# Group B's attention: which engine scales the first softmax map of each pair

## The chip, the cores and the metric

The kernel runs on one core of one Trainium2 chip. The metric is the device time of one execution in microseconds (us), the median of several runs. A core has five engines that matter here: TensorE (PE, with its weight loads as PEld), VectorE (DVE), ScalarE (ACT), GpSimd (POOL) and SyncE (SP), whose queue starts most of the DMAs. Each engine runs its own list of instructions in order and waits on semaphores for the others.

## The reference, cut to what matters

Two layers of an encoder step are computed for 1024 prompt frames (chunk-causal, chunks of 64) and 32 new frames behind 512 cached ones. Four head groups A, B, C and M read the same normed input. The change is in group B, differential attention: 4 heads, two softmax maps of 32-dim queries and keys for each head, 64-dim values.

```
ob = _full_attend(bq, bk, jnp.repeat(bv, 2, axis=2), B_SUB ** -0.5, q_start, prompt)
ob = ob.reshape(B, S, B_HEADS, 2, HEAD_DIM)
lam = exp(sum(lq1 * lk1)) - exp(sum(lq2 * lk2)) + lam_init
ob = _rms(ob[..., 0, :] - lam * ob[..., 1, :], b_subln_g) * (1.0 - lam_init)
```

So the output of a head is `softmax(map 0) @ v - lam * softmax(map 1) @ v`. The kernel forms the difference of the maps first, `P0 / sum0 - lam * P1 / sum1`, and multiplies it with the values once.

## The kernel before, in words

The kernel is a sequence of blocks with a barrier of all engines between them (`end_of_block`, L194). In each layer the groups M, B, A and C follow each other, each as a projection block (`pieces_block`) and an attention block (`attention_block`, L1004). Group B's attention runs twice, once in each layer.

An attention block goes through a list of jobs. For group B, `single_jobs` (L1294) makes 72 jobs: for each of the 8 prompt tiles of 128 frames, and for the tile of the 32 new frames, 8 jobs, one for each map. Jobs 2i and 2i+1 are the two maps of one head, a pair; there are 36 pairs in a layer. A job's keys are 128, 256, ... 1024 for the prompt tiles (4 pairs of each length) and 544 for the last tile (4 pairs). The order of work is written out by hand, one program for each engine, tied by semaphores:

- PE (L1076): scores of job j+2 (L1089), which wait until ScalarE has read the PSUM banks that they go to. Jobs of at most 512 keys have four such places and longer ones two. After an odd job it transposes the finished map of the pair (`turn`, L1104) and multiplies the transposed map of the pair before with the values (`values`, L1121).
- DVE (L1140): the mask and the negated row maximum of job j+1 (`maximum`, L1153 and L1163), then `divide(j)`. For an even job, `divide` is one reciprocal of the row sum (L1174), which signals `map_den`. For an odd job it is a reciprocal (L1183), a product with minus lambda (L1184), and, after a wait for `map_scaled`, the combination of both maps (L1186), which signals `p_ready`. Then comes the copy of an older output (`out_copy`, L1206).
- ACT (L1234): in an even step j, the exponential of job j+1 with its row sum (L1247), the scaling of map j (L1275, after a wait for `map_den`), the copies of the transposed maps from PSUM (L1263), and in the next step the exponential of job j+2.
- POOL (L1224): only for jobs of four heads (groups M and A) does it scale the maps (L1230). In group B's attention its program is empty.
- SP (L1281): sends each output tile to DRAM.

The tiles: `prob` holds the maps of four jobs, `rden` the reciprocals (element 0 of row 0 for the first map, of row 1 for the second), `pt` the transposed maps, `osb` the outputs, `nm` the negated maxima.

Of the kernel before, what the change touches and what calls it, by code (L numbers as in the profile page):

```python
# [19 lines left out]
ALU = mybir.AluOpType  # L20
# [24 lines left out]
def build_program(nc, I, O, consts):  # L45
# [958 lines left out]
    def attention_block(jobs, v_of, products, nk, start, pt_start=None, sinks=False, diff=False):  # L1004
# [7 lines left out]
        prob = w.take("prob", [P, 4, 1024])  # L1012
# [5 lines left out]
        rden = w.take("rden", [P, 2, 4])  # L1018
        osb = w.take("osb", [P, 4, 2 * P])
        NJ = len(jobs)  # L1020
# [3 lines left out]
        def segs(j):  # L1024

            jb = jobs[j]
            out = []
            for i in range(len(jb["heads"])):
                c = 0
                while c < jb["keys"]:  # L1030
                    n = min(P, jb["keys"] - c)
                    out.append((i, jb["tile0"] + c // P, i * 256 + c, n))
                    c += n
            return out

        def turn_groups(j):

            out, cur = [], []
            for n, sg in enumerate(segs(j)):
                if cur and (len(cur) == 4 or segs(j)[cur[0]][3] != sg[3]):  # L1040
                    out.append(cur)
                    cur = []
                cur.append(n)
            out.append(cur)
            return out
# [14 lines left out]
        def banks(j):  # L1060
            return [j % 4] if short(j) else [2 * (j % 2), 2 * (j % 2) + 1]
# [12 lines left out]
        with nc.Block() as block:  # L1074
            @block.tensor
            def _(pe):  # L1076
# [16 lines left out]
                def turn(p):  # L1093
                    j = pv_jobs[p]
                    r = jobs[j]["rows"]
                    pe.wait_ge(S.p_ready, p + 1)
                    sg = segs(j)
                    for n, grp in enumerate(turn_groups(j)):
                        g = first_group[p] + n
                        if g >= 2:  # L1100
                            pe.wait_ge(S.pt_copied, g - 1)
                        for i, b in enumerate(grp):
                            _, _, col, kn = sg[b]
                            last = pe.transpose(ps[0:kn, 4 + g % 2, i * P:i * P + r], prob[0:r, j % 4, col:col + kn],  # L1104
                                                ident[0:r, 0:r])
                        last.then_inc(S.pt_done, 1)

                def values(p):
                    j = pv_jobs[p]
                    r = jobs[j]["rows"]  # L1110
                    pe.wait_ge(S.pt_copied, first_group[p + 1])
                    if p >= 2:
                        pe.wait_ge(S.o_copied, p - 1)
                    sg = segs(j)
                    for i, h in enumerate(jobs[j]["heads"]):
                        mine = [n for n, x in enumerate(sg) if x[0] == i]
                        hp = jobs[j]["v_heads"][i]
                        part = 64 * (hp[0] % 2)
                        for m, b in enumerate(mine):
                            _, kt, _, kn = sg[b]  # L1120
                            last = pe.matmul(ps[part:part + 64, 6 + p % 2, (i // 2) * P:(i // 2) * P + r],  # L1121
                                             v_of(kt)[0:kn, 64 * hp[1]:64 * hp[1] + 64], pt[0:kn, p % 2, b, 0:r],
                                             start=(m == 0), stop=(m == len(mine) - 1))
                    last.then_inc(S.pv_done, 1)
# [98 lines left out]
            @block.gpsimd  # L1223
            def _(pool):  # L1224
                for j in range(NJ):
                    r, kn, nh = jobs[j]["rows"], jobs[j]["keys"], len(jobs[j]["heads"])
                    if nh > 1:
                        pool.wait_ge(S.den_ready, j + 1)
                        v = prob[0:r, j % 4, :].rearrange("p (h c) -> p h c", c=256)[:, :, 0:kn]
                        pool.tensor_tensor(v, v, rden[0:r, j % 2, 0:nh].unsqueeze(2).broadcast_to([r, nh, kn]),  # L1230
                                           ALU.mult).then_inc(S.p_ready, 1)

            @block.scalar
            def _(act):  # L1234
                def exponent(j):
                    jb = jobs[j]
                    r, kn, nh = jb["rows"], jb["keys"], len(jb["heads"])
                    act.wait_ge(S.nm_done, j + 1)
                    if j >= 4:
                        if diff and j % 2 == 0:  # L1240
                            act.wait_ge(S.p_ready, (j - 4) // 2 + 1)
                        else:
                            act.wait_ge(S.pt_done, first_group[sum(1 for q in pv_jobs if q <= j - 4)])
                    for i in range(nh):
                        col = i * 256
                        src = ps[0:r, banks(j)[0]:banks(j)[-1] + 1, :].rearrange("p a b -> p (a b)")[:, col:col + kn]
                        last = act.activation(prob[0:r, j % 4, col:col + kn], src, ACT.Exp, bias=nm[0:r, j % 4, i:i + 1],  # L1247
                                              accum_out=rsum[0:r, j % 4, i:i + 1])
                    if sinks:
                        last = act.activation(es[0:r, j % 2, :], es[0:r, j % 2, :], ACT.Exp)  # L1250
                    last.then_inc(S.exp_done, 1)

                def turned_copy(p):
                    j = pv_jobs[p]
                    r = jobs[j]["rows"]
                    sg = segs(j)
                    if p >= 2:
                        act.wait_ge(S.pv_done, p - 1)
                    for n, grp in enumerate(turn_groups(j)):
                        g = first_group[p] + n  # L1260
                        act.wait_ge(S.pt_done, g + 1)
                        kn = sg[grp[0]][3]
                        act.copy(pt[0:kn, p % 2, grp[0]:grp[0] + len(grp), 0:r],  # L1263
                                 ps[0:kn, 4 + g % 2, 0:len(grp) * P].rearrange("p (m c) -> p m c", c=P)[:, :, 0:r]
                                 ).then_inc(S.pt_copied, 1)

                exponent(0)
                p = 0
                for j in range(NJ + 1):
                    if j + 1 < NJ:  # L1270
                        exponent(j + 1)
                    if diff and j < NJ and j % 2 == 0:
                        r, kn = jobs[j]["rows"], jobs[j]["keys"]
                        act.wait_ge(S.map_den, j // 2 + 1)
                        act.mul(prob[0:r, j % 4, 0:kn], prob[0:r, j % 4, 0:kn], rden[0:r, 0, 0:1]).then_inc(S.map_scaled, 1)  # L1275
                    if p < NPV and pv_jobs[p] == j - 1:
                        turned_copy(p)
                        p += 1
# [864 lines left out]
```

## Time and profile before

| | |
|---|---|
| time, median of 3 runs (lowest to highest) | 3410.72 us (3407.08 to 3412.3) |
| span of the profiled execution | 3406.1 us |
| PE busy | 2985.7 us (88%) |
| PEld busy | 2776.2 us (82%) |
| DVE busy | 1793.5 us (53%) |
| ACT busy | 1407.6 us (41%) |
| POOL busy | 163.9 us (5%), 238 instructions |

The page gives the span of the profiled execution, from its first to its last instruction; no time of its own beside that span is given for it. The span is 4.6 us below the median. Shares are averages over all stages. Group B's attention is a stage of about 133 us in each layer, from 276.3 to 409.1 us and from 1949 to 2082 us; what ends last there has to be read from its own rows.

### The profile page before, as it was taken

The page shows a single profiled execution, that of the slowest core. Times are in us where ns is not written, and L with a number is a line of the kernel's source. Part 1 is how long each engine was busy: PE and PEld are TensorE (multiplying, and loading weights), DVE is VectorE, ACT ScalarE, POOL GpSimd, SP SyncE. Part 2 cuts the span into 40 slices and gives each one's busy share as a digit, 9 for nine tenths or more (in the row PEclk, how much of TensorE's full clock was granted, in tenths as well). Part 3 has the DMA queues.
Part 4 walks back from the last instruction along what each step waited for, and adds up shares of the span by engine and source line. Part 5 has one row for each costly group of instructions (what it writes and reads, how often), then busy time and mean ns, then how long its engine had stood idle before and what let it go on. Part 6 is the DMA issues. An engine that isn't in the chain of part 4 may idle for free. (4 is left out here: it accounts for less than half of the span.)

```text
span 3406.1 us, 50141 instructions
## 1 busy us (share of the span) xinstructions
PE 2985.7 (88%) x19244; PEld 2776.2 (82%) x19244; DVE 1793.5 (53%) x2837; ACT 1407.6 (41%) x2909; POOL 163.9 (5%) x238
## 2 busy tenths in 40 slices
PE   5787788797899999999967877797888999999997
PEld 3785577486799999999957856675687999999997
DVE  5366664664545444444564586456456444454444
ACT  5556644653242233222245575546423223222332
POOL 0100002100000000000002000120000000000000
PEclk8898889897899999999988998897998999999998
DMA  4110102004011111111031101110221111111111
GB/s 174 38 42 18 33 7 56 5 12 153 25 50 44 50 45 44 44 44 50 19 119 45 45 10 31 32 34 6 68 92 44 50 44 44 44 44 50 45 44 59
DMA packets 185839, 162.22 MB, mean 48 GB/s; under 512 B 17272, under 2 KB 172408, under 8 KB 185080
## 3 DMA queue, kind: packets, MB, share of 16 engines
q1 hardware_dynamic: 185592, 158.82, 14.9%
q8 instruction: 169, 2.77, 0.3%
q14 instruction: 78, 0.64, 0.1%
HBM read 129.92 MB, written 29.06 MB: 47 GB/s over the span
## 5 line engine op out<-in xcount | busy, mean ns | idle before, releaser
L1500 PE MATMUL ps<-h_hi,w_hi 128*128 128x352 f32 x2496 | 545.8, 327 | 50.3 <-DVE h_lo L317 22.6
L1500 PE MATMUL ps<-h_lo,w_hi 128*128 128x352 f32 x2496 | 541.6, 325 | 0.0
L1500 PE MATMUL ps<-h_hi,w_lo 128*128 128x352 f32 x2496 | 541.4, 324 | 0.0
L1500 PEld LDWEIGHTS ps<-h_hi,w_hi 128*128 128x128 f32 x2496 | 428.1, 190 | 57.6 <-issue 43.2
L1500 PEld LDWEIGHTS ps<-h_hi,w_lo 128*128 128x128 f32 x2496 | 431.6, 189 | 0.0
L1500 PEld LDWEIGHTS ps<-h_lo,w_hi 128*128 128x128 f32 x2496 | 428.3, 190 | 0.0
L697 PE MATMUL ps<-w_hi,h_hi 128*128 128x256 f32 (+1 forms) x1152 | 337.7, 293 | 68.8 <-DVE w_lo L853 64.0
L2004 DVE TENSOR_TENSOR x_t<-ps,x_t 128x1056 f32<-128x1056 f32 x176 | 221.0, 1255 | 289.5 <-PE ps L1500 288.8
L1980 DVE SCALAR_TENSOR_TENSOR cv<-up,cols,cv 128x1058 f32<-128x1058 f32 x88 | 116.1, 1319 | 477.7 <-ACT cv L1919 477.7
L698 PE MATMUL ps<-w_lo,h_hi 128*128 128x256 f32 (+1 forms) x1152 | 332.7, 289 | 0.0
L699 PE MATMUL ps<-w_hi,h_lo 128*128 128x256 f32 (+1 forms) x1152 | 330.4, 287 | 0.0
L1912 ACT COPY up<-ps 128x704 f32<-128x704 f32 x88 | 65.7, 746 | 591.4 <-PE ps L1500 591.4
L697 PEld LDWEIGHTS ps<-w_hi,h_hi 128*128 128x128 f32 (+1 forms) x1152 | 215.3, 187 | 73.3 <-DVE w_lo L853 48.4
L1089 PE MATMUL ps<-k_st,q_st 128*128 128x256 f32 (+9 forms) x768 | 195.8, 388 | 66.1 <-ACT prob L1247 44.5
L1247 ACT ACTIVATE prob<-ps,nm 128x256 f32<-128x256 f32 (+8 forms) x360 | 224.8, 638 | 58.9 <-DVE nm L1163 46.5
L1901 ACT CAST w_hi<-stage 128x1024 fp32r<-128x1024 f32 x132 | 135.9, 1043 | 241.5 <-PE ps L1500 240.8
L1500 PE MATMUL ps<-act_hi,w_hi 128*128 128x352 f32 x1056 | 229.4, 325 | 5.1 <-issue 5.1
L1500 PE MATMUL ps<-act_hi,w_lo 128*128 128x352 f32 x1056 | 229.0, 324 | 0.0
L1500 PE MATMUL ps<-act_lo,w_hi 128*128 128x352 f32 x1056 | 228.5, 325 | 0.0
L1089 PEld LDWEIGHTS ps<-k_st,q_st 128*128 128x128 f32 (+2 forms) x768 | 132.4, 225 | 113.2 <-ACT prob L1247 57.1
L699 PEld LDWEIGHTS ps<-w_hi,h_lo 128*128 128x128 f32 (+1 forms) x1152 | 216.0, 188 | 0.9
L698 PEld LDWEIGHTS ps<-w_lo,h_hi 128*128 128x128 f32 (+1 forms) x1152 | 215.3, 187 | 0.7
(174 smaller groups left out, 4555.7 us busy)
## 6 DMA issues: line engine op xcount, KB each, us to landing
stage<-in_f_win SPq DMA_DIRECT2D x88, 512.0 KB, 3.8
stage<-in_f_wout SPq DMA_DIRECT2D x44, 512.0 KB, 3.6
stage<-in_w_in SPq DMA_DIRECT2D x64, 256.0 KB, 4.0
x_spill<-x_t SPq DMA_DIRECT2D x2, 4224.0 KB, 13.7
o_in<-o_spill SPq DMA_DIRECT2D x8, 1056.0 KB, 9.4
x_t<-x_spill SPq DMA_DIRECT2D x2, 4224.0 KB
stage<-in_w_o SPq DMA_DIRECT2D x16, 512.0 KB, 5.2
x_in<-in_x_prompt SPq DMA_DIRECT2D x1, 4096.0 KB, 13.4
```

The costliest lines, as they stand in the source:

```text
L697: pe.matmul(out, h_hi[:, k, c:c + r], w_hi[:, k, :], start=(k == 0), stop=False)
L698: pe.matmul(out, h_hi[:, k, c:c + r], w_lo[:, k, :], start=False, stop=False)
L699: last = pe.matmul(out, h_lo[:, k, c:c + r], w_hi[:, k, :], start=False, stop=(k == KC - 1))
L1089: last = pe.matmul(out, q_st[0:nk, qb, q0:q0 + r], jb["k"][0:nk, jb["k_blk"] + kb, k0 + c:k0 + c + n], start=(m == 0), stop=(m == len(pair ...
L1247: last = act.activation(prob[0:r, j % 4, col:col + kn], src, ACT.Exp, bias=nm[0:r, j % 4, i:i + 1], accum_out=rsum[0:r, j % 4, i:i + 1])
L1500: last = pe.matmul(ps[:, s0 + b, 0:BAND], lh, rh_[:, b * BAND:(b + 1) * BAND], start=(first_k and n == 0), stop=(last_k and n == 2))
L1901: act.copy(w_hi[:, ws, :], stage[:, sg, :]).then_inc(S.hi_done, 1)
L1912: act.copy(up[:, b, 2:2 + 2 * BAND].rearrange("p (t c) -> p t c", c=BAND), ps[:, s0:s0 + 2, 0:BAND])
L1980: dve.scalar_tensor_tensor(cv[:, b, :], up[:, b, 1:UPC - 1], cols[:, 0, bass.ds(c + 2 * FC, 1)], cv[:, b, :], ALU.mult, ALU.add).then_inc( ...
L2004: dve.tensor_tensor(xm, ps[:, s0:s0 + 3, 0:BAND], xm, ALU.add).then_inc(S.x_added, 1)
```

## The change

The scaling of the first map of each pair moves from ScalarE's program to GpSimd's, as a `tensor_scalar` with the per-row reciprocal as its operand. It waits for the same semaphore and signals the same one. Nothing else is changed.

```diff
@@ pool program
                 for j in range(NJ):
                     r, kn, nh = jobs[j]["rows"], jobs[j]["keys"], len(jobs[j]["heads"])
+                    if diff and j % 2 == 0:
+                        pool.wait_ge(S.map_den, j // 2 + 1)
+                        pool.tensor_scalar(prob[0:r, j % 4, 0:kn], prob[0:r, j % 4, 0:kn], rden[0:r, 0, 0:1], None,
+                                           ALU.mult).then_inc(S.map_scaled, 1)
                     if nh > 1:
@@ act program
                     if j + 1 < NJ:
                         exponent(j + 1)
-                    if diff and j < NJ and j % 2 == 0:
-                        r, kn = jobs[j]["rows"], jobs[j]["keys"]
-                        act.wait_ge(S.map_den, j // 2 + 1)
-                        act.mul(prob[0:r, j % 4, 0:kn], prob[0:r, j % 4, 0:kn], rden[0:r, 0, 0:1]).then_inc(S.map_scaled, 1)
                     if p < NPV and pv_jobs[p] == j - 1:
```

## Rows read from the trace of the kernel before

**Rows 1.** Waits of DVE in B's attention, first layer: engine, line, waited-for, total us, times, longest.
```profile
DVE prob L1186 <- ACT prob L1275: 9.9, 20, 0.7
```
**Rows 2.** The same in B's attention of the second layer.
```profile
DVE prob L1186 <- ACT prob L1275: 10.0, 20, 0.8
```
**Rows 3.** Timeline, one pair of 1024 keys: start, us, engine, line, operation [idle before <-releaser].
```profile
376.15 1.22 DVE L1163 TENSOR_REDUCE nm<-ps 128x1 f32<-128x1024 f32 x1
376.29 0.74 PE L1089 MATMUL ps<-k_st,q_st 128*128 128x512 f32 x2 [1.40 <-ACT prob L1247]
...
377.29 0.15 DVE L1174 RECIPROCAL rden<-rsum 128x1 f32<-128x1 f32 x1
377.41 1.11 ACT L1247 ACTIVATE prob<-ps,nm 128x1024 f32<-128x1024 f32 x1 [1.17 <-DVE nm L1163]
...
377.59 1.23 DVE L1163 TENSOR_REDUCE nm<-ps 128x1 f32<-128x1024 f32 x1
...
378.51 1.14 ACT L1275 ACTIVATE prob<-prob,rden 128x1024 f32<-128x1024 f32 x1
...
378.92 0.16 DVE L1184 TENSOR_TENSOR rden<-rden,neglam 128x1 f32<-128x1 f32 x1
...
379.75 1.28 DVE L1186 SCALAR_TENSOR_TENSOR prob<-prob,rden 128x1024 f32<-128x1024 f32 x1 [0.67 <-ACT prob L1275]
380.49 1.13 ACT L1247 ACTIVATE prob<-ps,nm 128x1024 f32<-128x1024 f32 x1
...
381.51 1.22 DVE L1163 TENSOR_REDUCE nm<-ps 128x1 f32<-128x1024 f32 x1
```
**Rows 4.** Timeline, one pair of 512 keys.
```profile
312.82 0.15 DVE L1174 RECIPROCAL rden<-rsum 128x1 f32<-128x1 f32 x1
...
313.12 0.69 DVE L1163 TENSOR_REDUCE nm<-ps 128x1 f32<-128x512 f32 x1
...
313.92 0.16 DVE L1184 TENSOR_TENSOR rden<-rden,neglam 128x1 f32<-128x1 f32 x1
...
314.11 0.75 DVE L1186 SCALAR_TENSOR_TENSOR prob<-prob,rden 128x512 f32<-128x512 f32 x1
```
**Rows 5.** GpSimd's groups by shape: busy us, mean ns of one | idle before.
```profile
L1230 POOL TENSOR_TENSOR prob<-prob,rden 128x1024 f32<-128x1024 f32 x30 | 56.8, 1893 | 156.5 <-DVE rden L1179 156.5
L317 POOL TENSOR_TENSOR h_lo<-h,h_hi 128x1056 fp32r<-128x1056 f32 x12 | 29.2, 2432 | 187.9 <-ACT h_hi L312 187.9
...
L222 POOL TENSOR_SCALAR_AFFINE_SELECT ident<-ident 128x128 f32<-128x128 f32 x1 | 0.3, 292 | 0.2 <-POOL ident L220 0.2
...
L1797 POOL COPY conv_st<-up 128x4 f32 x80 | 15.2, 190 | 1343.8 <-ACT up L1915 1343.8
...
L1230 POOL TENSOR_TENSOR prob<-prob,rden 128x512 f32<-128x512 f32 x2 | 2.1, 1040 | 688.6 <-DVE rden L1179 688.6
```
**Rows 6.** Timeline, group M's attention: a reciprocal and the GpSimd scaling behind it.
```profile
130.85 0.18 DVE L1179 RECIPROCAL rden<-rsum 128x4 f32<-128x4 f32 x1 [0.29 <-ACT prob L1247]
...
131.11 1.89 POOL L1230 TENSOR_TENSOR prob<-prob,rden 128x1024 f32<-128x1024 f32 x1 [63.16 <-DVE rden L1179]
```
**Rows 7.** Timeline of GpSimd, group A's attention, second layer.
```profile
2191.90 1.89 POOL L1230 TENSOR_TENSOR prob<-prob,rden 128x1024 f32<-128x1024 f32 x1 [1.20 <-DVE rden L1179]
```
**Rows 8.** Timeline of DVE in the same stretch.
```profile
2191.18 0.16 DVE L1160 TENSOR_TENSOR nm<-mx,negsink 128x4 f32<-128x4 f32 x1
...
2192.89 0.92 DVE L1160 TENSOR_TENSOR nm<-mx,negsink 32x4 f32<-32x4 f32 x1
```
**Rows 9.** Timeline, first pairs of the 32-frame tile.
```profile
395.25 0.43 PE L1089 MATMUL ps<-k_s,q_st 128*32 128x512 f32 x2
...
395.72 0.71 DVE L1163 TENSOR_REDUCE nm<-ps 32x1 f32<-32x544 f32 x1 [0.34 <-PE ps L1089]
```
**Rows 10.** Timeline, end of B's attention and start of group A's projections.
```profile
412.25 2.08 SPq L622 DMA_DIRECT2D stage<-in_w_in  x4
...
415.10 1.30 ACT L747 CAST w_hi<-stage 128x512 fp32r<-128x512 f32 x2 [8.50 <-DMA stage<-in_w_in]
```
**Rows 11.** Instructions of line L222: ns min/median/max, first and last start.
```profile
L222 POOLq MODIFY_POOL_CONFIG  x2: 11/11/11, 1.1 to 1.1; - x2
```

## The prediction

> **What bounds the kernel now.** The page's busy shares say little: PE is busy 88% of the span, but the change touches two stages of 133 us each. I first asked the waits of DVE in group B's attention, then a timeline of one pair of long keys and of one of short keys, then GpSimd's rows by shape, and last what stands around the stage.
>
> The waits show one thing to look for: DVE's combination of the two maps (L1186) waits for ScalarE's scaling (L1275) in 20 of the 36 pairs of a layer, 9.9 us in the first layer and 10.0 us in the second [rows 1, 2]. The 20 are the pairs of 640, 768, 896, 1024 and 544 keys; in the 16 pairs of up to 512 keys it doesn't wait.
>
> In a pair of 1024 keys [rows 3] the period from maximum to maximum is 381.51 - 376.15 = 5.36 us. The cycle that sets it runs over two engines: maximum on DVE (376.15 to 377.37), exponential of the second map on ACT (377.41 to 378.52), scaling on ACT (378.51 to 379.65), combination on DVE (379.75 to 381.03), an output copy and a mask, and the next maximum. DVE's own list is otherwise without a gap, and it sits idle only 0.67 us before the combination. The scaling could have started much earlier: its reciprocal is done at 377.29 + 0.15 = 377.44, but ACT's program puts the exponential, 1.11 us, ahead of it. PE isn't the bound: it waits 1.40 us in the same pair for ScalarE to free the banks.
>
> In a pair of 512 keys [rows 4] the combination starts 0.03 us after the product with minus lambda ends (313.92 + 0.16 = 314.08, start 314.11). DVE alone sets the period there, and taking work from ACT buys nothing.
>
> **The change part by part.** It removes one ACT instruction and its wait from each of 72 pairs, and adds one GpSimd instruction to each. ACT's time by itself is worth nothing, since ACT isn't the bound; what counts is when the scaled map is ready.
>
> *What goes.* Without the wait, the combination starts 0.03 us after the product, as in the short pairs. What it waited includes this 0.03 us, so the stall that can go is 9.9 + 10.0 - 40 x 0.03 = 18.7 us. The exponential and the copies of transposed maps on ACT move up by the scaling's 1.14 us at 1024 keys; nobody late waits for them.
>
> *What is added.* GpSimd has nothing else in this stage. Its scaling starts when the first reciprocal is done. In group M the same handover took 131.11 - (130.85 + 0.18) = 0.08 us [rows 6]. At 1024 keys GpSimd would start at 377.44 + 0.08 = 377.52, while DVE makes the maximum of the next job, the second reciprocal and the product. The product starts at 378.92, so the cover is 1.40 us, which is that reduce (1.22) plus 0.18. At 512 keys it is 313.92 - 312.97 - 0.08 = 0.87 us, again the reduce (0.69) plus 0.18 [rows 4]. The reduce grows by (1.22 - 0.69) / 512 = 1.04 ns an element from 0.16 us, so the cover is 0.34 + 1.04 n, with n in thousands of keys. The combination can start 0.19 us after the product started; the handover from ACT takes 0.10 us (379.65 to 379.75), and I take the same for GpSimd. So the scaling may last 0.09 us longer than the cover before anything is late.
>
> *How long it lasts* is not in the trace: no GpSimd `tensor_scalar` with a per-row operand is there. From the rows, one bound is the two-input product on the same tile (L1230): 1893 ns at 1024 elements and 1040 at 512, that is 0.187 us + 1.67 ns an element [rows 5]. The dearer two-input row is L317, (2.43 - 0.19) / 1056 = 2.1 ns an element. The other side are the one-input rows: a copy of 4 elements takes 190 ns and the affine select of 128 takes 292, which is (292 - 190) / 124 = 0.82 ns an element. The new instruction reads one tile and a single scalar for each row, so the one-input rows are nearest, and I take 0.187 us + 0.82 to 1.2 ns an element: 1.03 to 1.42 us at 1024, against 1.49 allowed; 0.60 to 0.80 at 512, against 0.96; 0.29 to 0.34 at 128, against 0.56. Nothing is late. In general the scaling is late by (r - 1.04) n - 0.24 us at r ns an element, so up to r = 1.27 it costs nothing at any length. Below nothing it can't go: what is hidden can't be hidden more.
>
> The page "GPSIMD Engine Reference" of the Trainium skill (section Engine selection) says the same kind of thing: one-input elementwise work is roughly at line rate on GpSimd, two-input work about twice as slow as on VectorE. For two inputs the trace shows 1.89 us on GpSimd (L1230) against 1.28 on VectorE (L1186) at 1024 elements [rows 3, 5], 1.5 times; no row here shows GpSimd's `tensor_scalar`.
>
> *A port.* A DVE instruction with two SBUF inputs stood still beside GpSimd here: L1160 takes 0.16 us when GpSimd is idle, and 0.92 us, from 2192.89 to 2193.81, when GpSimd's L1230 runs from 2191.90 to 2193.79 [rows 7, 8]. The Trainium skill's page "SBUF — State Buffer" (section Who interferes with whom) has this as a lock: such an instruction and a GpSimd instruction that reads SBUF exclude each other, and the second one waits to the end. The product L1184 has two SBUF inputs too. If the scaling ends before it starts, as at the price that I take, it costs nothing. If the scaling is still running, the product ends about 0.02 us after it and the combination starts 0.03 us later, no later than by the 0.10 us of the handover. So the lock adds nothing to the formula. The combination itself never meets a scaling, as it waits for one and the next starts only behind the next maximum.
>
> *What is late next.* With the 0.64 us gone at 1024 keys, the period is 4.72 us, DVE's own work. PE had 1.40 us of idle in 5.36 and keeps 0.76. ACT's second exponential moves up with the removed scaling: it started at 380.49 and would start at about 379.5, so the scores behind it are done before the maximum that needs them. Only at the step to the 32-frame tile does PE bind: DVE already waits 0.34 us there for scores that PE puts behind the value products of the 1024-key tile [rows 9]. There the gain of one pair, about 0.35 us in each layer, is not had: 0.7 us in both.
>
> *What follows.* A barrier ends the stage, the weights of group A are only requested at 412.25 and ACT waits 8.50 us for them [rows 10]. All of that starts from the end of the stage and moves up whole.
>
> *The sum:* 18.7 - 0.7 = 18.0 us. The sum is made against the profiled span: 3406.1 - 18.0 = 3388.1. The median of the runs is 4.6 us above that span, and I take the step off it: 3410.7 - 18.0 = 3392.7, said as 3393.
>
> **Rivals.**
> 1. GpSimd's `tensor_scalar` costs as much as its two-input product, 1.67 ns an element. Then the lateness 0.63 n - 0.24 is 0.40, 0.32, 0.24, 0.16, 0.10 and 0.08 us at 1024, 896, 768, 640, 544 and 512 keys, together 1.30 us, times 8 pairs each is 10.4 us. Gain 18.0 - 10.4 = 7.6, time 3403. For it: the only large GpSimd rows on this tile are of this price. Against: they read two tensors, and the one-input rows have half the slope.
> 2. The stall is replaced at once by another, PE or ACT being nearly as late as the scaling: time unchanged, 3410.7. For it: two bank places only for long jobs, and PE occupied for 3.96 us of the 5.36. Against: PE's idle of 1.40 us is over twice the 0.64 taken away, and ACT loses more work than the cycle loses time.
> 3. Slower: the instruction on GpSimd is so slow that DVE waits for it longer than it did for ACT, and also in the pairs of 256 to 512 keys, which wait for nothing today. The point from which this decides is r where the lateness, summed over 384 to 1024 keys and 8 pairs each, eats 18.7 us: 8 x (4.77 (r - 1.04) - 1.68) = 18.7, r = 1.88. At the rate of L317, 2.1, the lateness 1.06 n - 0.24 sums to 3.4 us over the eight lengths that have one, times 8 is 27.3 us: 8.6 us slower, 3419. For it: that row exists, 2.43 us. Against: it writes another number type and reads two full tensors.
> 4. The instruction needs other code on GpSimd. The trace shows a configuration step ahead of the affine select, 11 ns on the queue at 1.1 us, with the select running at 1.2 us [rows 5, 11]: 0.1 us, nothing in the sum. The Trainium skill's page "GPSIMD Engine Reference" (section Instruction dispatch) gives about 6 us for the first call of a freshly loaded library; by that, an estimate, two stages would give back 12 us. The rows show copies, fills and products running without such a step, and I leave it inside the range.
>
> **Numbers.** Chances: forecast 0.62, rival 1 0.18, rival 2 0.10, rival 3 0.07, rival 4 0.03. A measurement of this kernel tells some 0.2%, 6.8 us, from no change, so faster means below 3403.9. Faster: 0.62 + 0.13 of rival 1 = 0.75. Same: 0.05 + 0.10 + 0.03 = 0.18. Slower: 0.07. The forecast by itself lies between 3388 (a little more than the stall, as ACT's copies come earlier) and 3398 (some pairs late by 0.1 us). The range takes in rival 1 and half of rival 2: 3387 to 3409.
>
> **What would show it.** In the profile of the changed kernel the waits of DVE in this stage should have no row of L1186 for GpSimd, or one under 1 us; the period at 1024 keys should be 4.7 us; GpSimd's new rows at 1024 keys should be under 1.49 us, starting 0.08 us after the first reciprocal; L1184 should stay at 0.16 us. Each stage should be 9 us shorter and nothing else should move. A GpSimd row of 1.9 us at 1024 keys with L1184 stretched to its end would be rival 1; over 2.1 us, rival 3. A new wait of L1163 for PE in most pairs would be rival 2.

## The result, and the profile after

The changed kernel takes 3438.7 us (median of 4 runs, 3437.5 to 3441.5) against 3411.4 us for the kernel before beside it. The ratio on record is 1.0088, with a 95% interval from 1.0074 to 1.0102: 25 to 35 us slower. (The quotient of these two medians is 1.0080, or 27 us; the ratios below, too, are those on record and not quotients of the medians shown.) The prediction said 3393, with a range of 3387 to 3409. It was wrong in size and in sign.

In the profile the span is 3437.5 us, 31.4 us more than before. All of it lies in the two stages of group B's attention. Measured from DVE's first maximum to the end of its last output copy, these took 132.3 us each before; now they take 148.3 and 147.4 us, 31.2 us more together before rounding. The rest of the span is 3141.5 us before and 3141.7 after.

The waits of DVE in the two stages (engine, line, waited-for, total us, times, longest) answer to [rows 1, 2]. First the first layer:

```profile
DVE prob L1186 <- POOL prob L1229: 25.5, 31, 1.5
DVE ps L1153 <- PE ps L1089: 4.5, 1, 4.5
```

and the second layer:

```profile
DVE prob L1186 <- POOL prob L1229: 25.5, 31, 1.5
DVE ps L1153 <- PE ps L1089: 4.3, 1, 4.3
```

The combination's wait for ScalarE is gone, as meant. In its place it waits for GpSimd, in 31 pairs of a layer where 20 waited before, and 25.5 us where it was 9.9 or 10.0. 51.0 - 19.9 = 31.1 us: the new waiting is the whole loss. (The row of L1153 is the wait for the first scores and lies ahead of the stage as measured here.)

The timeline of one pair of 1024 keys in the changed kernel (start, us, engine, line, operation) answers to [rows 3]. ScalarE's exponential is now at line L1251.

```profile
386.36 1.22 DVE L1163 TENSOR_REDUCE nm<-ps 128x1 f32<-128x1024 f32 x1
...
387.50 0.15 DVE L1174 RECIPROCAL rden<-rsum 128x1 f32<-128x1 f32 x1
387.62 1.11 ACT L1251 ACTIVATE prob<-ps,nm 128x1024 f32<-128x1024 f32 x1 [2.94 <-DVE nm L1163]
...
387.75 2.84 POOL L1229 TENSOR_SCALAR prob<-prob,rden 128x1024 f32<-128x1024 f32 x1 [3.26 <-DVE rden L1174]
...
389.14 0.16 DVE L1184 TENSOR_TENSOR rden<-rden,neglam 128x1 f32<-128x1 f32 x1
...
390.70 1.28 DVE L1186 SCALAR_TENSOR_TENSOR prob<-prob,rden 128x1024 f32<-128x1024 f32 x1 [1.40 <-POOL prob L1229]
...
392.46 1.23 DVE L1163 TENSOR_REDUCE nm<-ps 128x1 f32<-128x1024 f32 x1
```

GpSimd starts 0.10 us after the reciprocal, well ahead of where ScalarE started, and then takes 2.84 us for what ScalarE did in 1.14. It ends at 390.59, and DVE has been idle since its product ended at 389.30. The period is 392.46 - 386.36 = 6.10 us, where it was 5.36. ScalarE has more idle time than before (2.94 us ahead of the exponential, 1.17 in [rows 3]), and it buys nothing.

GpSimd's new groups by shape (busy us, mean ns of one | idle before) answer to [rows 5]:

```profile
L1229 POOL TENSOR_SCALAR prob<-prob,rden 128x1024 f32<-128x1024 f32 x8 | 22.7, 2842 | 25.8 <-DVE rden L1174 25.8
L1229 POOL TENSOR_SCALAR prob<-prob,rden 128x896 f32<-128x896 f32 x8 | 20.2, 2522 | 23.7 <-DVE rden L1174 23.7
...
L1229 POOL TENSOR_SCALAR prob<-prob,rden 128x512 f32<-128x512 f32 x8 | 12.5, 1563 | 15.8 <-DVE rden L1174 15.8
...
L1229 POOL TENSOR_SCALAR prob<-prob,rden 128x128 f32<-128x128 f32 x8 | 4.8, 603 | 254.2 <-DVE rden L1174 254.2
```

Two of these give the price: (2842 - 603) / 896 = 2.50 ns an element, with 0.28 us fixed. That is dearer than either price that the prediction drew from the trace for a rival, 1.67 and 2.1.

What follows the stage moved as a block: the weights of group A are requested at 426.68, where it was 412.25, and ScalarE again waits 8.5 us for them.

### The profile page after: what moved, and what is told of

It reads as the page before. It is cut to its first block and busy times, and to the rows that moved or that the text cites. A ratio compares the mean times of both kernels' runs of the same rounds, so it can differ in the third digit from the quotient of the medians.

```text
span 3437.5 us, 50141 instructions
## 1 busy us (share of the span) xinstructions
PE 3014.0 (88%) x19244; PEld 2790.5 (81%) x19244; DVE 1793.8 (52%) x2837; ACT 1364.0 (40%) x2837; POOL 287.2 (8%) x310
## 3 DMA queue, kind: packets, MB, share of 16 engines
q8 instruction: 169, 2.77, 0.3%
## 5 line engine op out<-in xcount | busy, mean ns | idle before, releaser
L1251 ACT ACTIVATE prob<-ps,nm 128x256 f32<-128x256 f32 (+8 forms) x360 | 225.2, 638 | 115.0 <-DVE nm L1163 101.2
```

## The experiments

Ten kernels were run. "Stage" is the length of the stage as above, in the profile of each; it was worked out for both layers and is 132.3 us before. It is the sharpest measure here, as the rest of the kernel differs by up to 13 us between the profiles, from 3139.4 us (e10_copy2) to 3152.3 (e4_copy). Times are medians, and the kernel before ran beside each. e2_quarter, e4_copy and e10_copy2 leave out part or all of the scaling and e3_const scales by a wrong number, so these four compute another result; the others are complete kernels.

| run | GpSimd at 1024 keys | stage, us | us | ratio to before (95%) |
|---|---|---|---|---|
| changed kernel | 2.84 | 148.3, 147.4 | 3438.7 | 1.0088 (1.0074 to 1.0102) |
| e1_tt | 1.89 | 127.6, 127.6 | 3401.6 | 0.998 (0.997 to 0.999) |
| e2_quarter | 0.92 | 123.0, 123.0 | 3394.7 | 0.9955 (0.9939 to 0.9972) |
| e3_const | 2.77 | 145.6, 144.5 | 3434.5 | one run |
| e4_copy | 1.04 | 123.1, 123.0 | 3400.2 | one run |
| e5_early | 2.84 | 126.6, 126.5 | 3396.8 | 0.9969 (0.9957 to 0.998) |
| e6_early_tt | 1.89 | 126.0, 126.1 | 3396.3 | 0.9965 (0.9951 to 0.9979) |
| e7_early_act | none | 127.3, 127.1 | 3398.9 | 0.9971 (0.996 to 0.9983) |
| e8_split | 1.56, half | 125.9, 126.1 | 3396.6 | 0.997 (0.9959 to 0.9981) |
| e9_split_tt | 1.47, three quarters | 123.5, 123.3 | 3390.3 | 0.9957 (0.9943 to 0.9971) |
| e10_copy2 | 2 x 1.04 | 134.4, 134.5 | 3410.1 | one run |

The theory to test was that the whole loss is the duration of one instruction, and that the rest of the prediction (which stall goes, what covers the scaling, what is late next) stands. The rival was that GpSimd beside DVE costs time whatever it does.

### Another instruction for the same product (e1_tt)

```diff
-pool.tensor_scalar(prob[0:r, j % 4, 0:kn], prob[0:r, j % 4, 0:kn], rden[0:r, 0, 0:1], None,
-                   ALU.mult).then_inc(S.map_scaled, 1)
+pool.tensor_tensor(prob[0:r, j % 4, 0:kn], prob[0:r, j % 4, 0:kn],
+                   rden[0:r, 0, 0:1].broadcast_to([r, kn]), ALU.mult).then_inc(S.map_scaled, 1)
```

> The changed kernel with GpSimd's tensor_scalar replaced by its two-input product (tensor_tensor, the reciprocal broadcast along the row), at the same place and with the same semaphores. Theory (the loss is the price of the one instruction: its rows read 0.283 us + 2.50 ns an element, 2.84 us at 1024): at 0.187 + 1.67 ns an element, 1.89 us at 1024, the combination is late by 0.63 n - 0.24 us, so the kernel is 8 us faster than before, 3403, with DVE's waits at L1186 near 11 us over both layers. If the port lock seen at L1160 holds for L1184 too, L1184 is stretched to the end of GpSimd's product (its row about 0.5 us at 1024 in place of 0.16), with no further cost. Rival (work on GpSimd beside DVE costs whatever the instruction, through the handovers or the shared port): still slower than before, 3420 or more, and DVE's other rows in the stage longer.

One call was changed, for the same result, and the kernel went from some 30 us slower to faster than before, by 0.1 to 0.3%; 9.4 us less over the two stages against 8 expected. The rival falls: work on GpSimd in this place isn't a cost by itself. DVE's long instructions keep their durations, too: in the first layer the maximum takes 751 or 752 ns and the combination 813 ns on average in every run here. Only L1184 is longer, 259 ns on average in place of 158. The expected wait of 11 us at L1186 was not there in name, as the port took it. The rows of one 1024-key pair:

```profile
371.85 1.22 DVE L1163 TENSOR_REDUCE nm<-ps 128x1 f32<-128x1024 f32 x1
...
373.22 1.89 POOL L1229 TENSOR_TENSOR prob<-prob,rden 128x1024 f32<-128x1024 f32 x1 [3.25 <-DVE rden L1174]
...
374.62 0.51 DVE L1184 TENSOR_TENSOR rden<-rden,neglam 128x1 f32<-128x1 f32 x1
...
375.21 1.28 DVE L1186 SCALAR_TENSOR_TENSOR prob<-prob,rden 128x1024 f32<-128x1024 f32 x1
...
376.98 1.22 DVE L1163 TENSOR_REDUCE nm<-ps 128x1 f32<-128x1024 f32 x1
```

The product L1184 lasts until 375.13 (0.16 us otherwise), GpSimd's until 375.11. The wait for the scaled map now sits inside a busy row of 0.51 us instead of in an idle gap, so the list of waits shows none of it.

### A quarter of the columns (e2_quarter)

```diff
+kq = kn // 4
-pool.tensor_scalar(prob[0:r, j % 4, 0:kn], prob[0:r, j % 4, 0:kn], rden[0:r, 0, 0:1], None,
+pool.tensor_scalar(prob[0:r, j % 4, 0:kq], prob[0:r, j % 4, 0:kq], rden[0:r, 0, 0:1], None,
```

> The changed kernel with only the first quarter of each map's columns scaled on GpSimd (the rest of the map stays unscaled, work left out). Theory (once the scaling is shorter than its cover nothing is late): at 2.5 ns an element it lasts 0.283 + 0.64 = 0.92 us at 1024 keys, under the 1.49 allowed, so the whole 18.0 us of the prediction's sum are there: 3393, period at 1024 keys 4.72 us, no wait of L1186 for GpSimd. Rival (another wait takes the stall's place at once, PE's scores or ACT's exponentials): 3405 to 3411, with new DVE waits for PE or ACT of 10 us or more in the two stages.

The stages are 9.3 us shorter each, 18.7 us together. The time is 15 us less by the ratio (10 to 21), and the sum of the prediction, 18.0, lies in that interval. There is no wait at L1186, and the period at 1024 keys is 378.18 - 373.44 = 4.74 us:

```profile
373.44 1.23 DVE L1163 TENSOR_REDUCE nm<-ps 128x1 f32<-128x1024 f32 x1
...
374.83 0.93 POOL L1230 TENSOR_SCALAR prob<-prob,rden 128x256 f32<-128x256 f32 x1 [3.81 <-DVE rden L1174]
...
376.41 1.28 DVE L1186 SCALAR_TENSOR_TENSOR prob<-prob,rden 128x1024 f32<-128x1024 f32 x1
...
378.18 1.22 DVE L1163 TENSOR_REDUCE nm<-ps 128x1 f32<-128x1024 f32 x1
```

So the rest of the prediction holds: which stall goes, that DVE's own 4.7 us is the next limit, and that neither PE nor ACT takes its place.

### What makes tensor_scalar dear (e3_const, e4_copy)

```diff
# e3_const
-pool.tensor_scalar(prob[0:r, j % 4, 0:kn], prob[0:r, j % 4, 0:kn], rden[0:r, 0, 0:1], None,
+pool.tensor_scalar(prob[0:r, j % 4, 0:kn], prob[0:r, j % 4, 0:kn], 0.5, None,
# e4_copy
-pool.tensor_scalar(prob[0:r, j % 4, 0:kn], prob[0:r, j % 4, 0:kn], rden[0:r, 0, 0:1], None,
-                   ALU.mult).then_inc(S.map_scaled, 1)
+pool.tensor_copy(prob[0:r, j % 4, 0:kn], prob[0:r, j % 4, 0:kn]).then_inc(S.map_scaled, 1)
```

> The changed kernel with a constant 0.5 in place of the per-row reciprocal as GpSimd's operand (the first map is scaled by the wrong number). Theory (the price is the per-row operand, read again for every element beside the tile): the slope falls from 2.50 to about 1.7 ns an element or less, 1.9 us or less at 1024, and the kernel comes to about 3403 or lower. Rival (the price is tensor_scalar's own loop with its two operation slots): rows as in the changed kernel, 2.84 us at 1024, and 3438.

> The changed kernel with a plain one-input copy of each map onto itself on GpSimd in place of the scaling (no scaling at all, work left out). Theory of the prediction, kept for copies: one-input rows go at 0.82 ns an element, 1.03 us at 1024, and the kernel at 3393. Rival (no elementwise GpSimd instruction on this tile is faster than the product): 1.67 ns an element or more, 1.9 us or more at 1024, and 3403 or later. It tells whether the one-input rows were too small to be drawn out to 1024 elements, or whether tensor_scalar is the exception.

GpSimd's groups with the constant:

```profile
L1229 POOL TENSOR_SCALAR prob<-prob 128x1024 f32<-128x1024 f32 x8 | 22.2, 2770 | 25.7 <-DVE rden L1174 25.7
...
L1229 POOL TENSOR_SCALAR prob<-prob 128x128 f32<-128x128 f32 x8 | 4.2, 531 | 257.4 <-DVE rden L1174 257.4
```

and with the copy:

```profile
L1229 POOL COPY prob<-prob 128x1024 f32<-128x1024 f32 x8 | 8.3, 1042 | 29.5 <-DVE rden L1174 29.5
...
L1229 POOL COPY prob<-prob 128x128 f32<-128x128 f32 x8 | 2.4, 295 | 256.7 <-DVE rden L1174 256.7
```

The theory on the operand falls: reading it costs 0.07 us an instruction and nothing an element, the slope stays (2770 - 531) / 896 = 2.50 ns. The copy has (1042 - 295) / 896 = 0.83 ns and 0.19 us fixed, which is what the prediction had drawn from a copy of 4 elements and a select of 128. So the line through the small rows was good, for copies. It was the wrong instruction's line. Three instructions of GpSimd on the same tile cost 0.83 (copy), 1.67 (product of two tensors) and 2.50 ns an element (`tensor_scalar`), 1 to 2 to 3. Why the one with fewer inputs is the slower of the two products was not settled.

e4_copy's one execution took 3400.2 us where 3393 was expected, although its stages are 18.5 us shorter. The rest of that execution is 10.8 us longer than in the profile of before; why is not known, and it lies outside the change.

### An earlier start (e5_early, e6_early_tt)

```diff
 for j in range(NJ):
+    if diff and j % 2 == 0 and j:
+        divide(j)
     while seen <= upto(j, 1):
         maximum(seen)
         seen += 1
-    divide(j)
+    if not diff or j % 2 == 1 or j == 0:
+        divide(j)
```

> The changed kernel (tensor_scalar on GpSimd) with one move on DVE: the reciprocal of an even job is made before the maximum of the next job, not after it. Theory (the loss is only that the scaling outlasts its cover): GpSimd starts one reduce earlier, the cover grows to two reduces, the combination could start 0.90 + 2.08 n us behind the reciprocal and the scaled map is there at 0.46 + 2.50 n, which is never later up to 1024 keys. So the loss is gone and the stall of before too: 17 us faster than before, 3394, period at 1024 keys 4.75 us with the 2.84 us rows of GpSimd unchanged. A small new wait of DVE at the reciprocal for ACT's exponential, about 0.1 us a pair, may take 3 to 7 us of it. Rival (GpSimd's long instructions slow DVE down by themselves, through the shared port): still no faster than before, 3411 or more.

> Both: the two-input product on GpSimd and the reciprocal ahead of the next maximum. Theory: nothing is late and L1184 no longer meets GpSimd (product 1.89 us against some 2.8 us to L1184), so its rows are back at 0.16 us, and the time is that of the run before this one within 2 us, 3393, as GpSimd's speed no longer counts. Rival: if the instruction's speed counts still, it is faster than the tensor_scalar variant by 5 us or more.

With the slow `tensor_scalar` in place, 2.84 us as in the changed kernel, moving one reciprocal on DVE turns 31 us of loss over the stages into a gain of 11.4 us. The rival falls: GpSimd may be as slow as that if its cover is long enough. One pair of 1024 keys of e5_early:

```profile
372.82 0.16 DVE L1174 RECIPROCAL rden<-rsum 128x1 f32<-128x1 f32 x1
372.99 0.11 DVE L1153 MEMSET ps<- 64x64 f32 x1
373.08 2.84 POOL L1232 TENSOR_SCALAR prob<-prob,rden 128x1024 f32<-128x1024 f32 x1 [2.02 <-DVE rden L1174]
...
376.03 1.28 DVE L1186 SCALAR_TENSOR_TENSOR prob<-prob,rden 128x1024 f32<-128x1024 f32 x1
...
377.70 0.16 DVE L1174 RECIPROCAL rden<-rsum 128x1 f32<-128x1 f32 x1
```

GpSimd ends at 375.92 and the combination starts at 376.03 without idle. The gain expected was 17 us, or 3 to 7 us less with a small new wait for ScalarE's exponential. 11.4 us came, but that wait is the smaller part of what is missing. These stages are 3.6 us longer each than e2_quarter's. 1.3 us of it are waits in the list that e2_quarter hasn't: 0.5 for GpSimd, in the last pair of 512 keys, 0.2 and 0.3 for the exponentials at the two reciprocals, and 0.3 ahead of one combination. Most of the rest I had not seen, and it has to do with what stands ahead of the reciprocal:

```profile
367.77 0.28 DVE L1206 COPY osb<-ps 64x128 f32<-64x128 f32 x1
367.98 0.14 DVE L1174 RECIPROCAL rden<-rsum 128x1 f32<-128x1 f32 x1
368.13 0.11 DVE L1153 MEMSET ps<- 64x64 f32 x1
...
372.50 0.29 DVE L1206 COPY osb<-ps 64x128 f32<-64x128 f32 x1
```

In the old place the reciprocal starts 0.08 us before the end of the maximum ahead of it, and the mask follows 0.08 us behind that maximum. In the new place, behind an output copy, it is so in about every second pair (367.98 to 368.13). In the others, 17 in the first layer, it starts 0.03 us or more behind the copy (372.82), and the mask follows 0.20 us behind the copy: 0.12 us more, 2.0 us in a layer. Why the pairs take turns was not tested. The faster instruction of e6_early_tt takes about 0.5 us off a stage, the wait in that pair of 512 keys.

### The same order without GpSimd (e7_early_act)

```diff
 for j in range(NJ + 1):
-    if j + 1 < NJ:
-        exponent(j + 1)
     if diff and j < NJ and j % 2 == 0:
         ...
         act.mul(...)
+    if j + 1 < NJ:
+        exponent(j + 1)
```

(together with DVE's early reciprocal)

> No GpSimd at all: the kernel before with the reciprocal ahead of the next maximum and ScalarE's scaling ahead of the exponential of the second map, so that it falls in ACT's idle time of 1.17 us at 1024 keys. Theory: the order is what mattered, not the engine; ACT then has 1.14 + 1.20 + 1.05 + 1.20 = 4.6 us of work in a period of 4.9 us, so about 0.4 of the 0.64 us go at 1024 keys and 8 to 12 us in all: 3401. Rival (ACT must be relieved): no faster than before, as the exponential of the second map only starts behind the scaling and DVE's second reciprocal waits for it.

10.2 us less over the stages: as expected (0.3% faster). The times are not to be told from those of the two runs with GpSimd, whose stages give 11.4 and 12.5 us. ScalarE's scaling falls into what was its idle time ahead of the exponential. The engine mattered little; where in the order the scaling starts mattered much.

### Sharing the map (e8_split, e9_split_tt)

```diff
# e8_split (at L1173 the count waited for is doubled in the same way)
+kh = kn // 2
+pool.wait_ge(S.map_den, j // 2 + 1)
+pool.tensor_scalar(prob[0:r, j % 4, 0:kh], prob[0:r, j % 4, 0:kh], rden[0:r, 0, 0:1], None,
+                   ALU.mult).then_inc(S.map_scaled, 1)
...
-act.mul(prob[0:r, j % 4, 0:kn], ...).then_inc(S.map_scaled, 1)
+act.mul(prob[0:r, j % 4, kn // 2:kn], ...).then_inc(S.map_scaled, 1)
...
-dve.wait_ge(S.map_scaled, j // 2 + 1)
+dve.wait_ge(S.map_scaled, 2 * (j // 2 + 1))
# e9_split_tt: kh = 3 * kn // 4, tensor_tensor in place of tensor_scalar, the last quarter on ScalarE
```

> The kernel before with the scaling shared: GpSimd's tensor_scalar takes the first half of the columns, ScalarE keeps the second half at its old place, and DVE waits for both. Theory: GpSimd's half, 0.283 + 1.25 n us, is within its cover but for 0.07 us at 1024 keys; ACT's half ends about 0.43 n us sooner than the whole did, so the stall falls by 0.44, 0.39, 0.33, 0.28 and 0.23 us at 1024, 896, 768, 640 and 544 keys, 13 us in all: 3398. Rival (any tensor_scalar on GpSimd costs DVE time): 3406 or more.

> A complete kernel built from what the runs showed: GpSimd's two-input product takes the first three quarters of the columns of the first map, ScalarE keeps the last quarter at its old place. GpSimd: 0.187 + 1.25 n us, 1.47 at 1024 keys against 1.49 allowed. ACT: a quarter ends about 0.64 n us sooner than the whole, 0.66 at 1024 against the 0.64 of the stall. Theory (the only limits are these two durations, then DVE's own work): each stage 123.2 us in place of 132.3, as in the run that scaled a quarter only, 18 us in all, ratio 0.9947, 3390 beside a kernel before of 3408. Rival (sharing one map between two engines costs a further wait, or the early-order variants' 11 us are the floor for a complete kernel): 126 us a stage, ratio 0.9965 or more.

Half and half gives 12.6 us over the stages against 13 expected, with `tensor_scalar` still in it. Three quarters by GpSimd's product and one by ScalarE gives 17.8 us over the stages, and 3390.3 us against 3406.1 for the kernel before: 0.3 to 0.6% faster. It is the fastest complete kernel here, and its stages are within about 0.5 us of the run that left three quarters of the scaling out. In its 1024-key pair GpSimd and ScalarE end together, and DVE doesn't wait:

```profile
371.21 1.47 POOL L1230 TENSOR_TENSOR prob<-prob,rden 128x768 f32<-128x768 f32 x1 [3.27 <-DVE rden L1174]
...
372.20 0.50 ACT L1280 ACTIVATE prob<-prob,rden 128x256 f32<-128x256 f32 x1
...
372.61 0.16 DVE L1184 TENSOR_TENSOR rden<-rden,neglam 128x1 f32<-128x1 f32 x1
...
372.80 1.28 DVE L1186 SCALAR_TENSOR_TENSOR prob<-prob,rden 128x1024 f32<-128x1024 f32 x1
```

### Which instructions exclude each other (e10_copy2)

```diff
# against e4_copy
+pool.tensor_copy(prob[0:r, j % 4, 0:kn], prob[0:r, j % 4, 0:kn]).then_inc(S.pool_step, 1)
+pool.wait_ge(S.pool_step, j // 2 + 1)
 pool.tensor_copy(prob[0:r, j % 4, 0:kn], prob[0:r, j % 4, 0:kn]).then_inc(S.map_scaled, 1)
```

> The run with plain copies on GpSimd, with two copies one behind the other for each first map (the scaling itself is left out), so that a one-input GpSimd instruction is under way when DVE's two-input product L1184 starts (second copy from about 1.2 to 2.2 us behind the reciprocal at 1024 keys, L1184 at 1.5). If any GpSimd instruction that reads SBUF locks out a DVE instruction with two SBUF inputs, L1184's mean rises well above 0.16 us, to 0.6 or more at 1024 keys. If only two-input GpSimd instructions do, as tensor_scalar's rows suggest, it stays at 0.16. Either way the second copy makes the combination late by about 0.7 us at 1024 keys, and the kernel lands near that of before, 3405 to 3415.

```profile
381.32 1.04 POOL L1231 COPY prob<-prob 128x1024 f32<-128x1024 f32 x1
...
381.64 0.73 DVE L1184 TENSOR_TENSOR rden<-rden,neglam 128x1 f32<-128x1 f32 x1
```

The stages are 2.1 and 2.3 us longer than before, as expected. L1184 lasts from 381.64 to 382.37, the copy to 382.36; over the 32 pairs of 128 rows in the first layer its mean is 432 ns. So a one-input copy shuts DVE's two-input product out as well, and my guess from `tensor_scalar`'s rows, that it takes a two-input GpSimd instruction, is wrong. In the changed kernel L1184 stays at 0.16 us in all pairs, though GpSimd's `tensor_scalar` runs from 387.75 to 390.59 around it. What sets `tensor_scalar` apart is open.

## Why the prediction was wrong

- **What bounds the stage**: right. The cycle over DVE and ACT, the 0.67 us of idle, and DVE's own 4.72 us as the next limit all came out; e2_quarter has 4.74 us a period.
- **What goes**: right, 18.7 us of stall. The same run shortened the stages by 18.7 us, and e4_copy by 18.5. The 0.7 us that the sum took off for PE at the first 32-frame pair were not there in it: DVE waited 0.3 us for those scores in each layer, as before. In e9_split_tt it waited 0.7.
- **What is added, the cover**: right. GpSimd's handover was 0.10 us for 0.08. The formula allowed 1.49 us at 1024 keys, the run at 1.04 us was not late, and the one at 1.89 was, by about the 0.4 us that it gives (the period is 5.13 us from 371.85 to 376.98 in e1_tt's rows, against 4.74 in e2_quarter's).
- **How long it lasts**: this is the step that failed. I took "0.187 us + 0.82 to 1.2 ns an element" because the instruction reads one tile, and it costs 0.28 us + 2.50 ns. With that price the prediction's own formula gives a lateness of 0.283 + 2.50 n - (0.34 + 1.04 n) - 0.09 = 1.46 n - 0.15 us; over the nine lengths (5.15 thousand keys together) and 8 pairs each that is 8 x (7.52 - 1.32) = 49.6 us. Less the 18.7 us that go, the kernel is 30.9 us slower; the stages measured 31.2. One mis-sized term accounts for all of it.
- **The bounds**: the second fault. I said that no row showed the operation, and then took the nearest rows above it, 1.67 and 2.1 ns, as the ends of what could be. I had the break-even price, 1.88 ns, which lies between these two rows, and gave 7% to all that lies beyond it. For an instruction without a row that was far too little.
- **A port**: the lock was seen in the right place, and was harmless as worked out (e1_tt's 5.13 us is the 4.72 and the 0.40 of the formula without it), but with the instruction of this change it didn't act at all. The Trainium skill's page "SBUF — State Buffer" (section Who interferes with whom) has it for any GpSimd instruction that reads SBUF. The copy and the two-input product agree (0.73 and 0.51 us in place of 0.16); `tensor_scalar` doesn't, with 0.16 us under 2.84 us of it.
- **The rule on prices**: the rule of the Trainium skill's page "GPSIMD Engine Reference" (section Engine selection), one-input work roughly at line rate, holds for the copy: 0.83 ns an element, where DVE's maximum takes 1.04. For `tensor_scalar`, which reads one tensor too, the measurement is three times that, and the measurement decides.
- **Rival 3** named the mechanism that came true, with its place and the point from which it decides; its size, 8.6 us, was too small by the same term.
- **Rivals 2 and 4**: neither came. e2_quarter has no new wait in the stall's place. No configuration step of GpSimd stands at L1229 in the changed kernel's trace, and its first scaling took 0.61 us where the next three of 128 keys took 0.60.
- **What follows, and what is late next**: right but for those 0.7 us. DVE has no wait for PE in most pairs, and the rest of the kernel moved whole.

## What to carry to other kernels

Price an instruction by a row of that very instruction on that very engine; a row of another operation with the same inputs bounded nothing here (0.83, 1.67 and 2.50 ns an element for three that look alike). When no row exists, work out the price at which the change breaks even first, and let the chances follow from how far the known rows lie from it. And when an engine waits for a short helper step, ask what starts it before asking who runs it: here an earlier start was worth about as much with ScalarE (10.2 us over the stages) as with a GpSimd instruction 2.5 times as slow (11.4).

## What the runs showed of the hardware that was not expected

- GpSimd's `tensor_scalar` in float32 costs 2.50 ns an element and 0.28 us with a per-row operand, 0.21 us with a constant, while its `tensor_tensor` with the same operand broadcast costs 1.67 ns and 0.19 us.
- DVE's two-input product stood still beside a GpSimd copy or two-input product, and ran in its usual 0.16 us beside `tensor_scalar`. Such a wait shows as a longer busy row of DVE and in no list of waits: in e1_tt the row read 0.51 us and L1186 had no wait.
- What a small DVE instruction costs depends on what stands ahead of it. A reciprocal of a single column started 0.08 us before the end of a long maximum, and before the end of every second output copy; behind the other copies it started 0.03 us after the end, and cost 0.12 us more.
